# Two gate projections of each merge tile as seven block products, in three of four chunks of a gated mixer layer on one core

## The chip, the cores and the metric

The kernel runs on one core of a Trainium2 chip. Its time is the device time of one execution in microseconds. Three runs of the kernel before gave 2286.47, 2287.43 and 2288.08 us, median 2287.43 us. The engines are named as in the profile: PE is TensorE (PEld its weight loads), DVE is VectorE, ACT is ScalarE, POOL is GpSimd, SP is SyncE, which issues nearly all DMAs here.

## What is computed

One layer over x of 2048 tokens by 1024 channels, all in float32. A norm of the rows, one wide projection, three token mixers (a 31-tap convolution, differential attention with 4 heads, a 3-tap gated convolution), and then the merge, which is the part of this case:

```python
h = rmsnorm(x, norm_g[l])
proj = h @ w_in[l]
(a_val, a_gate, a_z, q, k, v, b_z, c_b, c_c, c_x, c_z, gates) = jnp.split(proj, SPLIT_IDX, axis=-1)
...                       # y_a, y_b, y_c: outputs of the mixers, each (tokens, 1024)
g = jax.nn.sigmoid(gates + gate_b[l]).reshape(b, s, N_BRANCH, D_MODEL)
merged = g[:, :, 0] * y_a + g[:, :, 1] * y_b + g[:, :, 2] * y_c
x = x + merged @ w_o[l]
...
return rmsnorm(x, final_g)
```

The gates are three times 1024 columns of the wide projection, with 1024 channels to sum over.

## The kernel before

Everything is held turned: channels on the 128 partitions, tokens along the row. The 2048 tokens are done in four chunks of 512 (chunk 0 to 3). A product in float32 is made of three products of a faster format: each operand is split into a high part (a rounded copy, by ACT) and a low part (the rest, by DVE or POOL), and high*high, high*low and low*high are summed in one PSUM bank. One weight tile (1024 channels to 128 outputs) is thus 8 blocks of channels by 3 products, 24 matmuls with 512 columns each, in one bank of PSUM.

**Steps.** Each engine runs a program written out by hand over the same clock of steps: 88 weight tiles in a chunk, 6 steps to a tile, 528 steps in a chunk, 4 matmuls of 512 columns to a step (`PARTS`, `SPAN`, L52 to L62). Whatever is to be done at step p stands in each engine's program at step p, and semaphores hold the engines together. The tiles of a chunk are: 44 of the heads (steps 0 to 263, with the attention put in between), 8 of gate a (264 to 311), 8 merge tiles of three weight tiles each (312 to 455, `MID_AT`, 18 steps to each), 4 of y_a (456 to 479, `YA_AT`), 8 of the output projection (480 to 527, `FIN_AT`).

**A merge tile** m makes 128 channels of gate b (24 matmuls), 128 of gate c (24), and then y_b and y_c (12 each, 512 channels to sum over). `row_part` (L790) does the gates into the two banks `PJ`; ACT reads each bank with a tanh into `TG` (`gate`, L1125), and DVE multiplies with the y products and sums into `merged` (`product`, L1615).

**Weights.** In chunk 0 each tile comes raw into `Wraw`, is split by ACT (`split_hi`) and by POOL or DVE (`split_lo`) into one of three slots of `Wp`, and is stored split to DRAM (`store_split`, 1 MB). In the other chunks `load_split` (L616) brings it back, one load of 1 MB for each tile, issued when the tile three before is used up.

**Other work that matters here.** The 124 taps of the long convolution run on DVE, `HEAD_TAPS` (L362) of them spread over steps 40 to 264 and the rest before the layer norm at `LN_AT` (L223). POOL does small powers and a few splits. At `XN_AT` (L236, step 444) the rows of the next chunk are squared by ACT, at `XS_AT` (460) PE spreads their scales, from `XT_AT` (461) on DVE and ACT make the normed and split input `hT`. The rows come in with `load_x` at XN_AT - 8 and XN_AT - 4, into the rooms of `UC` and `SZA`, which the branch of y_a must have left (`za_lo`). Keys and values (`KM`, `VM`) are used by the attention until about step 300 and by the output projection from step 456; the score banks `SC` are free between them.

Of the kernel before, what the change touches and what calls it, by code (L numbers as in the profile page):

```python
# [49 lines left out]
W_SLOTS = 3  # L50
# [17 lines left out]
BANK_CHUNK = G_CHUNK // 2  # L68
# [7 lines left out]
def bank_use(c, r):  # L76

    return BANK_CHUNK * c + r // 2
# [14 lines left out]
def weight_slot(c, i):  # L93
    return (W_CHUNK * c + i) % W_SLOTS


def last_group(i):

    if i < W_MID:
        return i  # L100
    if i < W_YA:
        m, k = divmod(i - W_MID, 3)
        return G_MID + 4 * m + (k if k < 2 else 3)
    return G_YA + 2 * (i - W_YA) + 1

# [94 lines left out]
OSUM_LAG = (10, 10, 10, 9)  # L200
# [9 lines left out]
DIRECT_SPREAD = (19, 15, 15, 15)  # L210
# [12 lines left out]
LN_AT = (408, 408, 408, 414)  # L223
# [6 lines left out]
LN_SPREAD_AT = 13  # L230
# [5 lines left out]
XN_AT = 444  # L236
XS_AT = 460

XT_LOADS = 4
XT_LOAD_AT = 451  # L240
XT_LOAD_STEP = 6
XRES_STEP = 4
XT_AT = 461
# [6 lines left out]
YA_AT = PARTS * W_YA  # L250
FIN_AT = PARTS * W_FIN
# [58 lines left out]
SPARE = 14  # L310
# [27 lines left out]
def room_table(c):  # L338


    free = [(r, None) for r in range(SPARE if c == 0 else 4 * KB)]
# [17 lines left out]
    return room, [(r, done) for p, done, r in gates]  # L359


HEAD_TAPS = (58, 46, 24, 0)  # L362
HEADS_FROM = 40
HEADS_TO = 264
AFTER_FROM = 268
# [54 lines left out]
def build(nc, x, x_t, w_stream, cols, final_g, lam_v, out, kd, vd, ws, rs):  # L420
    with ExitStack() as ctx:
# [17 lines left out]
        xres = PX[:, 1, :, :, :].rearrange("p t m n -> p t (m n)")  # L439
        ZA = sb("ZA", [P, 2, KB, CHUNK], F32R)  # L440
# [6 lines left out]
        Wraw = sb("Wraw", [P, 2, D])  # L447
        Wp = sb("Wp", [P, W_SLOTS, 2, D], F32R)
# [16 lines left out]
        LT = [SZB[:, :], Y[:, :], ACC2, VT]  # L465
        identf = sb("identf", [P, P])
# [33 lines left out]
        w_loaded = [sem(f"w_loaded{k}") for k in range(2)]  # L500
        w_stored = [sem(f"w_stored{k}") for k in range(W_SLOTS)]
        w_back = [sem(f"w_back{k}") for k in range(W_SLOTS)]
# [11 lines left out]
        tanh_done = sem("tanh_done")  # L514

# [42 lines left out]
        def pair_rooms(c):  # L558


            if c > 0:
                return [Wraw[:, 0, k * 2 * P:(k + 1) * 2 * P] for k in range(4)]
            return [room(SPARE + k // 2)[:, k % 2 * 2 * P:(k % 2 + 1) * 2 * P] for k in range(4)]


        OV = Wraw[:, 1, 0:2 * P]
# [18 lines left out]

        def pj(c, r):
            return FIRST_BANKS[r] if c == 0 and r < 2 else PJ[bank(r)]
# [6 lines left out]
        def weight_used(eng, c, i):  # L594

            if i < W_FIN:
                eng.wait_ge(group_done, G_CHUNK * c + last_group(i) + 1)
            elif i < W_CHUNK - 1:
                eng.wait_ge(fin_done, FIN_SIGNALS * c + i - W_FIN + 1)
            else:  # L600
                eng.wait_ge(fin_done, FIN_SIGNALS * (c + 1))
# [4 lines left out]
        def _(sp):  # L606
            def load_raw(w):
                wait(sp, w_lo, w - 1)
                sp.dma_start(Wraw[:, w % 2, :], w_stream[w, :, :]).then_inc(w_loaded[w % 2], 16)

            def store_split(w):
                k = w % W_SLOTS
                sp.wait_ge(w_lo, w + 1)
                sp.dma_start(ws[w, :, :, :], Wp[:, k, :, :].bitcast(F32)).then_inc(w_stored[k], 16)

            def load_split(c, i):  # L616
                k, before = weight_slot(c, i), W_CHUNK * c + i - W_SLOTS
                weight_used(sp, before // W_CHUNK, before % W_CHUNK)
                if before < W_CHUNK:
                    sp.wait_ge(w_stored[k], 16 * (before // W_SLOTS + 1))  # L620
                if c == 1:
                    sp.wait_ge(w_stored[i % W_SLOTS], 16 * (i // W_SLOTS + 1))
                sp.dma_start(Wp[:, k, :, :].bitcast(F32), ws[i, :, :, :]).then_inc(w_back[k], 16)
# [68 lines left out]
            for w in range(W_SLOTS):  # L692
# [1157 lines left out]
```

## Time and profile before

| | |
|---|---|
| median of three runs | 2287.43 us |
| the profiled execution | 2287.08 us, span of its trace 2285.3 us, granted clock 0.999 |
| PE matmul busy | 2258.3 us, 10822 matmuls |
| DVE, ACT, POOL busy | 1425.9, 756.3, 232.9 us |
| DMA | 493.53 MB, mean 216 GB/s |
| chunk 0, 1, 2, 3 begin at about | 14, 540, 1085, 1664 us; the last matmul ends at 2276 |

The page gives busy shares of each engine, the chain of work that ended last, and groups of instructions. Matmuls are pipelined, and so the duration of one (about 390 ns at 512 columns) is longer than the distance from one start to the next; prices of PE are taken from distances.

### The profile page before, as it was taken

The numbers are of one execution on the slowest core, as the hardware profiler recorded it, in microseconds if no ns is written. First come the engines' busy times: TensorE is split into PE (matmuls) and PEld (weight loads), VectorE is DVE, ScalarE is ACT, GpSimd is POOL, SyncE is SP. The second block draws the span as 40 slices with busy tenths as digits, with TensorE's granted clock in tenths as the row PEclk, the third lists the DMA queues.
The fourth block names the chain that finished last, engine by engine and source line by source line (L and its number), as shares of the span: only waits on it lengthen the run. The fifth ranks groups of instructions, "written<-read, shape, count | busy, mean of one in ns | idle before, by whom it ended". The sixth has DMA issues, their size and how long they took to land.

```text
span 2285.3 us, 29046 instructions
## 1 busy us (share of the span) xinstructions
PE 2258.3 (99%) x10822; PEld 1833.4 (80%) x10822; DVE 1425.9 (62%) x2706; ACT 756.3 (33%) x1610; POOL 232.9 (10%) x186
## 2 busy tenths in 40 slices
PE   7999999999999999999999999999999999999998
PEld 6888888878888888888788788888877787788886
DVE  4767667774666675554566667665546656677752
ACT  4334332342333331021344344102135445441121
POOL 3544400100000000010000000001000000000010
PEclk9999999999999999999999999999999999999999
DMA  8877788788566665566655565556775555545555
GB/s 312 287 267 265 269 289 290 273 326 325 163 202 196 180 153 193 200 241 249 258 182 173 171 195 159 169 187 239 262 260 143 174 163 168 158 135 184 187 192 201
DMA packets 99339, 493.53 MB, mean 216 GB/s; under 512 B 15360, under 2 KB 18304, under 8 KB 54144
## 3 DMA queue, kind: packets, MB, share of 16 engines
q1 hardware_dynamic: 90464, 488.90, 63.9%
q10 hardware_dynamic: 8736, 2.78, 0.6%
q8 instruction: 87, 1.43, 0.3%
q14 instruction: 52, 0.43, 0.1%
HBM read 378.37 MB, written 113.27 MB: 215 GB/s over the span
## 4 chain that ended last, share of the span: by engine, by line
PE 95%; DVE 2%; DMA 1%; issue 1%; ACT 1%; SPq 0%; DVEq 0%; ACTq 0%
PE PJ L768 74%; PE SC L827 6%; PE SC L859 5%; PE TB L868 3%; PE OB L892 1%; PE OB L893 1%; PE OB L827 1%; PE PJ L827 1%; PE OB L895 1%; PE OB L894 1%; PE TB L903 0%; DMA PX<-x_t 0%; DMA UC<-x 0%; PE TB L919 0%; DVE Wp L1341 0%
## 5 line engine op out<-in xcount | busy, mean ns | idle before, releaser
L768 PE MATMUL PJ<-hT,Wp 128*128 128x512 f32 x6480 | 1571.6, 394 | 0.5 <-DVE PX L1631 0.5
L768 PEld LDWEIGHTS PJ<-hT,Wp 128*128 128x128 f32 x6480 | 1189.5, 188 | 254.2 <-issue 17.7
L1551 DVE SCALAR_TENSOR_TENSOR ACCS<-UA,col,ACCS 128x512 f32<-128x512 f32 x464 | 350.7, 798 | 0.4
L1065 ACT ACTIVATE PX<-SC,negm 128x512 f32<-128x512 f32 (+3 forms) x320 | 196.2, 623 | 145.7 <-DVE negm L1380 143.8
L1425 DVE TENSOR_TENSOR ZA<-TB,ZA 128x512 fp32r<-128x512 f32 (+1 forms) x144 | 95.1, 661 | 176.9 <-ACT ZA L1085 176.0
L1380 DVE TENSOR_REDUCE negm<-SC 128x2 f32<-128x1024 f32 (+3 forms) x160 | 169.0, 1062 | 40.2 <-PE SC L859 37.6
L1085 ACT ACTIVATE ZA<-TB 128x512 fp32r<-128x512 f32 (+1 forms) x144 | 82.7, 574 | 322.1 <-PE TB L868 322.1
L1136 ACT ACTIVATE TG<-PJ,col 128x512 f32<-128x512 f32 x64 | 44.1, 689 | 348.1 <-PE PJ L768 348.0
L1418 DVE SCALAR_TENSOR_TENSOR PX<-PX,sc 128x512 f32<-128x512 f32 (+3 forms) x160 | 108.1, 696 | 51.0 <-ACT PX L1076 50.8
L827 PE MATMUL SC<-Wp,KM 128*128 128x512 f32 x384 | 121.4, 389 | 0.0
L1076 ACT ACTIVATE PX<-PX,sc 128x512 f32<-128x512 f32 (+3 forms) x160 | 98.9, 655 | 64.9 <-DVE sc L1407 44.6
L1245 POOL TENSOR_TENSOR Wp<-Wraw,Wp 128x1024 fp32r<-128x1024 f32 x42 | 106.2, 2529 | 126.6 <-ACT Wp L990 126.6
L859 PE MATMUL SC<-KM,ZA 64*128 64x512 f32 (+3 forms) x960 | 118.5, 379 | 0.0
L990 ACT ACTIVATE Wp<-Wraw 128x1024 fp32r<-128x1024 f32 x88 | 92.8, 1055 | 59.8 <-DMA Wraw<-w_stream 34.6
L859 PEld LDWEIGHTS SC<-KM,ZA 64*128 64x128 f32 x960 | 80.3, 184 | 39.2 <-issue 28.7
L768 PE MATMUL PJ<-ZC,Wp 128*128 128x512 f32 x384 | 93.2, 390 | 2.5 <-ACT TG L1136 2.5
L768 PE MATMUL PJ<-ZB,Wp 128*128 128x512 f32 x384 | 92.7, 390 | 0.0
L768 PE MATMUL PJ<-ZA,Wp 128*128 128x512 f32 x384 | 89.1, 391 | 1.7 <-DVE CT L1631 0.9
L768 PEld LDWEIGHTS PJ<-ZC,Wp 128*128 128x128 f32 x384 | 71.8, 188 | 17.7 <-issue 2.9
L768 PEld LDWEIGHTS PJ<-ZA,Wp 128*128 128x128 f32 x384 | 71.6, 188 | 17.5 <-DVE Wp L1341 2.0
L768 PEld LDWEIGHTS PJ<-ZB,Wp 128*128 128x128 f32 x384 | 72.1, 188 | 15.4 <-issue 0.5
L827 PEld LDWEIGHTS SC<-Wp,KM 128*128 128x128 f32 x384 | 72.1, 188 | 14.9
(192 smaller groups left out, 2038.5 us busy)
## 6 DMA issues: line engine op xcount, KB each, us to landing
Wp<-split_weights SPq DMA_DIRECT2D x264, 1024.0 KB, 4.8
split_weights<-Wp SPq DMA_DIRECT2D x88, 1024.0 KB, 4.9
Wraw<-w_stream SPq DMA_DIRECT2D x88, 512.0 KB, 5.9
KM<-keys SPq DMA_DIRECT2D x24, 512.0 KB, 5.9
VM<-values SPq DMA_DIRECT2D x24, 512.0 KB, 6.4
PX<-x SPq DMA_DIRECT2D x16, 512.0 KB, 7.8
out<-PX SPq DMA_DIRECT2D x16, 512.0 KB, 10.6
keys<-KM SPq DMA_DIRECT2D x12, 512.0 KB, 9.6
```

Of the source, the lines that this page charges most:

```text
L768: mm = pe.matmul(pj(c, r)[:, :], wt, rhs[:, 1 if q == 1 else 0, k, :], start=(n == 0), stop=(n == 3 * ktiles - 1))
L827: mm = pe.matmul(FIN_BANKS[half][t], (mTl if q == 1 else mTh)[:, k, t * P:(t + 1) * P], Wp[:, weight_slot(c, w), 1 if q == 2 else 0, kk * ...
L859: mm = pe.matmul(SC[k][:, m, 0:w], QM[rows, ql, t * P:(t + 1) * P], KM[rows, kl, j * CHUNK:j * CHUNK + w], start=(n == 0), stop=(n == 2))
L990: act.activation(Wp[:, k, 0, :], Wraw[:, w % 2, :], ACT.Copy).then_inc(w_hi, 1)
L1065: a = act.activation(probs(c, h, t, j, m)[:, 0:w], SC[k][:, m, 0:w], ACT.Exp, bias=negm[:, t % 2, j, m:m + 1], accum_out=lsum[:, t % 2, j, ...
L1076: act.activation(probs(c, h, t, j, 0)[:, 0:w], probs(c, h, t, j, 0)[:, 0:w], ACT.Copy, scale=sc[:, t % 2, j, 0:1]).then_inc(half_done, 1)
L1085: act.activation(AT[:, u % 2, 0, 0:w], TB[:, 0:w], ACT.Copy).then_inc(at_hi, 1)
L1245: pool.tensor_tensor(Wp[:, k, 1, :], Wraw[:, w % 2, :], Wp[:, k, 0, :].bitcast(F32), ALU.subtract).then_inc(w_lo, 1)
L1380: dve.tensor_reduce(negm[:, t % 2, j, :], SC[k][:, :, 0:w], AX.X, ALU.max, negate=True).then_inc(negm_ready, 1)
L1418: dve.scalar_tensor_tensor(out=probs(c, h, t, j, 0)[:, 0:w], in0=probs(c, h, t, j, 1)[:, 0:w], scalar=sc[:, t % 2, j, 1:2], in1=probs(c, h ...
L1425: dve.tensor_tensor(AT[:, u % 2, 1, 0:w], TB[:, 0:w], AT[:, u % 2, 0, 0:w].bitcast(F32), ALU.subtract).then_inc(tb_free, 1)
L1551: a = dve.scalar_tensor_tensor(out=acc, in0=src, scalar=col[:, n:n + 1], in1=acc, op0=ALU.mult, op1=ALU.add)
```

## The change

For chunks 1 to 3 the two gates of a merge tile are one product of a 2 by 2 block matrix of weights (two gates by two halves of the 1024 channels) with a 2 by 2 block matrix of the input (two halves of the channels by two halves of the 512 tokens). It is now made of seven block products in place of eight (Winograd's form): each product is 4 blocks of channels by 3 splits, 12 matmuls of 256 columns. Four of the seven need sums of weight blocks (S1 to S4), four need sums of blocks of the input. Chunk 0 keeps the plain products.

- PE: `gates_part`, 7 matmuls of 256 columns to a step in place of 4 of 512; the products lie in the score banks. y_b and y_c are as before.
- DVE: `add_quarter`, seven adds of 128x256 for each merge tile, with one operand in PSUM, into `TG`; ACT copies the first product to SBUF (`copy_first`), and the tanh reads `TG`.
- Weight sums: in chunk 1, steps 24 to 272, 32 sums: DVE adds 128x512, ACT and POOL split, SP stores 512 KB each to `wsum`; raw weights are loaded for it (256 KB halves).
- Weight blocks: slots are halves now (six of 512 KB); S1 to S4 and y come back as 512 KB loads, the three plain blocks of each merge tile come raw (256 KB) and are split by ACT and POOL. Chunk 0 no longer stores the 16 gate tiles.
- Sums of the input: steps 508 to 519 of chunks 0 to 2: DVE four adds and four splits of 1024 elements to a partition, ACT four copies; stored (2 x 2 MB) at steps 20 and 40 of the next chunk, loaded back into the rooms of keys and values after the attention (at 272 and about 305), in pieces of 256 elements.
- Places: layer norm of chunk 0 at 400, of chunk 3 at 408 (before 408 and 414); norm of the next input at 452 in chunk 0 and 448 in the next two (before 444), its spread at 468 in chunk 0; more taps among the heads in chunks 1 to 3.

```diff
-LN_AT = (408, 408, 408, 414)
+LN_AT = (400, 408, 408, 408)
-LN_SPREAD_AT = 13
+LN_SPREAD_AT = 15
-XN_AT = 444
-XS_AT = 460
+XN_AT = (452, 448, 448, 0)
+XS_AT = (468, 460, 460, 0)
-XT_LOAD_AT = 451
+XT_LOAD_AT = (459, 451, 451, 0)
-XT_AT = 461
+XT_AT = (469, 461, 461, 0)
+RAW_AT = ((0, 0, -14), (0, 1, -13), (1, 1, -9))
+SPLIT_AT = ((A11, -6), (A12, -5), (A22, 0))
+QUARTER_AT = (6, 7, 7, 10, 10, 12, 12)
+BLOCK_AT = ((S1, -9), (S2, -7), (S3, -3), (S4, 0), (YB, 4), (YC, 6))
+SUM_AT = 24
+SUM_STEP = 8
+SUMS_AT = 508
+SUMS_STORE_AT = (20, 40)
+X_LOAD_AT = (442, 444)
+SUMS_BACK_AT = 272
-HEAD_TAPS = (58, 46, 24, 0)
+HEAD_TAPS = (58, 72, 78, 50)
...
+            def store_sum(m, k):
+                sp.wait_ge(sum_lo, 4 * m + k + 1)
+                sp.dma_start(wsum[m, SUM_ORDER[k], :, :, :], SS[:, :, :].bitcast(F32)).then_inc(sum_stored, 16)
...
+            def load_block(c, m, k):
+                q, i = mid_block(m, k), W_MID + 3 * m + 2
+                s = block_slot(c, q)
+                slot_free(sp, c, q)
...
+                sp.dma_start(Wp[:, s, :, :].bitcast(F32), src).then_inc(w_back[s], 16)
...
+            def load_sums(c, k):
+                if k == 0:
+                    sp.wait_ge(qk_done, units_before(c + 1))
+                else:
+                    sp.wait_ge(pv_done, turns_before(c + 1))
...
+                for half in range(2):
+                    a = slice(HALF * half, HALF * (half + 1))
+                    for l in range(2):
+                        sp.dma_start((TS, TU)[k][:, l, :, a].bitcast(F32), tz[k if half == 0 else 1 - k, :, l, :, a]
+                                     ).then_inc(t_back[k], 16)
...
+            def gates_part(c, m, part):
+                n0 = merge_at(c, m)
+                for n in range(PRODUCTS * part, PRODUCTS * (part + 1)):
+                    b, i = divmod(n, 3 * KB)
+                    k, q = divmod(i, 3)
+                    if i == 0:
+                        weight_ready(c, mid_block(m, b))
...
+                        elif b == S3:
+                            pe.wait_ge(p1_copied, n0 + 1)
+                            if m == 0:
+                                pe.wait_ge(t_back[1], 64 * c)
+                        elif b == S4:
+                            pe.wait_ge(quarter_done, PRODUCTS * n0 + 1)
+                        elif b == A22:
+                            pe.wait_ge(quarter_done, PRODUCTS * n0 + 3)
...
+                    mm = pe.matmul(P_BANKS[b], Wp[:, block_slot(c, mid_block(m, b)), 1 if q == 2 else 0, k * P:(k + 1) * P], rows,
+                                   start=(i == 0), stop=(i == 3 * KB - 1))
...
+            def block_hi(c, m, b):
+                q, half = mid_block(m, b), raw_of(m, b)
+                slot_free(act, c, q)
+                raw_loaded(act, c, *half)
+                act.activation(Wp[:, block_slot(c, q), 0, :], raw_home(c, *half), ACT.Copy).then_inc(w_hi, 1)
+            def sum_high(m, k):
+                act.wait_ge(sum_ready, 4 * m + k + 1)
+                wait(act, sum_stored, 16 * (4 * m + k))
...
+                act.activation(SS[:, 0, :], sum_home(m, SUM_ORDER[k]), ACT.Copy).then_inc(sum_hi, 1)
+            def copy_first(c, m):
...
+                act.activation(P1[:, :], P_BANKS[A11], ACT.Copy).then_inc(p1_copied, 1)
...
+            def add_quarter(c, m, k):
+                n = merge_at(c, m)
+                b, src, dst, after = ((S2, P1[:, :], C22, 0), (S1, C22, C12, 1), (A12, P1[:, :], C11, 0), (S3, C22, C21, 1),
+                                      (S1, C21, C22, 4), (S4, C12, C12, 2), (A22, C21, C21, 4))[k]
+                dve.wait_ge(prod_done, PRODUCTS * n + b + 1)
...
+                dve.tensor_tensor(dst, P_BANKS[b], src, ALU.add).then_inc(quarter_done, 1)
...
-                        if p == MID_AT + MID_STEPS * m + PARTS:
+                        if p == MID_AT + MID_STEPS * m + (PARTS if c == 0 else 2 * PARTS - 1):
                             gate(c, m, 1)
...
+                        for k in range(4):
+                            if c == 1 and p == SUM_AT + SUM_STEP * (4 * m + k):
+                                weight_sum(m, k)
+                    for n in range(4):
+                        if c + 1 < NCHUNK and p == SUMS_AT + 2 * n:
+                            turned_sums(c + 1, n)
+                        if c + 1 < NCHUNK and p == SUMS_AT + 5 + 2 * n:
+                            sums_lo(c + 1, n // 2, n % 2)
```

The store of a weight sum stands in SP's program five steps after DVE's sum, ACT's copy and POOL's rest one step after it, the next sum eight steps after it.

## Rows read from the trace of the kernel before

**Rows 1.** The page, parts 1 and 2: busy time, and TensorE's clock in 40 slices.

```profile
PE 2258.3 (99%) x10822; PEld 1833.4 (80%) x10822; DVE 1425.9 (62%) x2706; ACT 756.3 (33%) x1610; POOL 232.9 (10%) x186
...
PEclk9999999999999999999999999999999999999999
```

**Rows 2.** The page, part 4: the chain that ended last, by engine.

```profile
PE 95%; DVE 2%; DMA 1%; issue 1%; ACT 1%; SPq 0%; DVEq 0%; ACTq 0%
```

**Rows 3.** Waits of PE, whole span: us in total, times, longest us.

```profile
PE TB L839 <- DVE SZB L1353: 8.8, 3, 7.8
PE OB L768 <- DVE hT L1369: 3.3, 2, 2.6
PE PJ L768 <- ACT TG L1136: 2.5, 1, 2.5
...
PE PJ L768 <- DVE Wp L1341: 0.8, 1, 0.8
```

**Rows 4.** The chain in order of time: a piece of chunk 1's merge stage.

```profile
887.59 85.24 PE PJ L768 x376
```

**Rows 5.** Timeline of PE: 256-column matmuls of the attention and what follows (start, us).

```profile
595.63 0.28 PE L894 MATMUL OB<-ZA,VM 128*128 128x256 f32 x1
...
595.86 2.01 PE L768 MATMUL PJ<-hT,Wp 128*128 128x512 f32 x8
...
2065.87 0.28 PE L894 MATMUL OB<-ZA,VM 128*128 128x256 f32 x1
...
2066.11 2.91 PE L768 MATMUL PJ<-hT,Wp 128*128 128x512 f32 x12
```

**Rows 6.** Timeline of PE's weight loads around such a pair.

```profile
1726.58 0.19 PEld L895 LDWEIGHTS OB<-ZA,VM 128*128 128x128 f32 x1
1726.69 1.69 PEld L768 LDWEIGHTS PJ<-hT,Wp 128*128 128x128 f32 x8
```

**Rows 7.** Timeline: end of chunk 0, load of rows, the two engines behind it.

```profile
458.01 2.31 SPq L630 DMA_DIRECT2D UC<-x  x2
...
466.45 1.06 ACT L995 ACTIVATE ACCS<-UC 128x1024 f32<-128x1024 f32 x1 [4.59 <-DMA UC<-x]
...
467.50 0.67 ACT L1136 ACTIVATE TG<-PJ,col 128x512 f32<-128x512 f32 x1
```

**Rows 8.** Groups by form, whole span: busy us, mean ns of one.

```profile
L1551 DVE SCALAR_TENSOR_TENSOR ACCS<-UA,col,ACCS 128x512 f32<-128x512 f32 x464 | 350.7, 798 | 0.4
...
L1431 DVE TENSOR_TENSOR Wraw<-Wraw,OB 128x256 f32<-128x256 f32 x24 | 10.1, 420 | 27.3 <-ACT Wraw L1094 27.1
...
L1276 POOL TENSOR_TENSOR ZA<-UC,ZA 128x512 fp32r<-128x512 f32 x16 | 23.8, 1501 | 58.4 <-ACT ZA L1152 58.4
```

**Rows 9.** Windows: PE, PEld, DVE, ACT, POOL busy (instructions), clock, DMA share, GB/s.

```profile
540.00:842.00 302.00, 302.00 (x1499) 244.77 (x1499) 189.69 (x432) 102.62 (x261) 16.88 (x20) 1.00 0.63 195
...
1664.00:2040.00 376.00, 375.64 (x1970) 298.12 (x1969) 238.10 (x501) 181.40 (x454) 19.76 (x21) 1.00 0.56 173
889.00:1020.00 131.00, 131.00 (x579) 107.64 (x578) 73.72 (x131) 22.16 (x37) 9.53 (x10) 1.00 0.58 211
...
1020.00:1042.00 22.00, 22.00 (x103) 18.36 (x102) 18.58 (x29) 6.33 (x10) 0.00 (x0) 1.00 0.74 264
```

**Rows 10.** Timeline, chunk 0: a POOL split and a tiny DVE operation beside it.

```profile
105.38 2.49 POOL L1245 TENSOR_TENSOR Wp<-Wraw,Wp 128x1024 fp32r<-128x1024 f32 x1 [4.73 <-ACT Wp L990]
...
105.72 2.16 DVE L1410 TENSOR_TENSOR sc<-Lr,lamv 128x2 f32<-128x2 f32 x1
```

**Rows 11.** The line of the 512 KB stores values<-VM, whole span.

```profile
DMA to landing us min/median/max: 3.4/4.5/8.5
```

**Rows 12.** DMA issues in 1004 to 1022 us: us to landing.

```profile
UC<-x SPq DMA_DIRECT2D x2, 512.0 KB, 7.4
```

**Rows 13.** Timeline, heads of chunk 1: turned weights ready on DVE, and PE's use.

```profile
628.35 0.69 DVE L1425 TENSOR_TENSOR ZA<-TB,ZA 128x512 fp32r<-128x512 f32 x1 [2.94 <-ACT ZA L1085]
...
631.17 0.39 PE L892 MATMUL OB<-ZA,VM 128*128 128x512 f32 x1
```

## What the change will do to the time: the prediction

> **What bounds the kernel now.** I read the page first. TensorE is busy for 99% of the span at the full clock (2.4 GHz) in every slice, DVE for 62% [rows 1], and 95% of the chain that ended last is TensorE [rows 2]. A chain of one engine has two ways to get shorter: fewer starts, or fewer waits. So the next view is the list of TensorE's waits: 8.8 us of DVE's first scales, nearly all of it at the start of the program, 3.3 us for the first rows, and then, in over 2250 us, only some 5 us, most of it one wait of 2.5 us and one of 0.8 us at the end of chunk 0 [rows 3]. The time is therefore the sum of TensorE's start distances, and a saved matmul is saved time unless a new wait takes its place. All sums below are made against the profiled execution, 2287.08 us (its span is 2285.3); the median of the three runs is 2287.43, 0.35 us above it, so that no correction is made.
>
> **Price of a matmul.** At 512 columns, from the chain in the merge stage of chunk 1: 85.24 us / 376 = 0.2267 us from start to start [rows 4]. At 256 columns the trace has pairs in the attention (lines 894 and 895), followed at once by a projection. From the start of line 894 to that of the projection, two starts on, are 0.23 us at the first of them and 0.24 at the last; of 108 such pairs 64 show 0.24 and 44 show 0.23, a mean of 0.2359, so 0.1180 us for one [rows 5]. That is more than half of 0.2267 (0.1134). Each needs its own weight load, and the loads of such a pair begin 0.11 us apart though each is shown with 0.19 [rows 6]: loads overlap each other, and 0.118 can be held in a long row of them, for which the trace has no example beyond a pair.
>
> **Term 1, the products.** Removed in each merge tile: 48 matmuls of 512 columns, 48 x 0.2267 = 10.88 us. Added: 84 of 256, 84 x 0.1180 = 9.91 us. Gain 0.97 us, in 8 tiles of 3 chunks: 24 x 0.97 = 23.3 us, all of it on the path. One eighth of the arithmetic is gone (24 x 1.36 = 32.6 us at half price), but nearly a third of that goes back for the narrower form. Bounds: 0.1134 us (half of the wide one) gives 32.6 us; 0.1226 us, as far above the mean as the half lies below it, gives 24 x (10.88 - 10.30) = 13.9 us.
> The Trainium skill (TensorE: Matmul & The Clock Gate, section Back-to-back issue gap) puts the distance at columns / 2.4 GHz plus 2.5 ns, so 109 ns and 216 ns. By it the term would be 24 x (48 x 0.2158 - 84 x 0.1092) = 28.5 us; the rows show 10 ns more at either width, and the sum above doesn't use the rule.
>
> **Term 2, the end of chunk 0.** The load of the last two row tiles was issued at 458.01, ScalarE waited for it until 466.45, and the tanh of a gate queued behind it began at 467.50 [rows 7]; this is TensorE's wait of 2.5 us, and 0.8 us follow on a late weight split [rows 3]. With the squares eight steps later (7 us) and the layer norm eight earlier, the load has 12 steps (11 us) from issue to use in place of 8, against 8.4 us seen. Gain 3.3 us (0 to 4.2, the last with the two waits of 0.5 us on products in the same place).
>
> **Term 3, what is added, and its cover.**
> DVE's adds. Seven of 128x256 with one operand in PSUM, 0.42 us each (line 1431 has this form) [rows 8], 2.9 us in a merge tile. Per chunk 56 x 0.42 = 23.5 us; out of the stage go 26, 54 or 50 taps of 0.80 us (21, 43, 40 us), so its sum on DVE grows by 3 us in chunk 1 (to some 76 of 124 us) and falls in the others [rows 8, 9]. TensorE waits for the adds only at the sixth product (first add, at step 6, used at 8.6) and the seventh (third add, step 7, used at 10.3), about 2 us of room. That suffices outside the layer norm. At steps 423 to 435 DVE has in addition four applies (1.2 us each) and four products (1.4 to 1.5 us each), with the adds of tile 6 some 14 us of work in 10 us: it falls behind by about 4 us, and the third add of tile 6 comes perhaps 0.5 us late. 3 x 0.5 = 1.5 us (0 to 6).
> POOL's splits. Three of 128x512 in each merge tile, 1.5 us each [rows 8], and 32 in the heads of chunk 1. Beside a POOL operation a DVE operation on two numbers took 2.16 us, until POOL was done [rows 10]. If half of a split's length falls on DVE, that is 24 x 0.75 = 18 us in a merge stage, in all 94 of 124 us in chunk 1, 76%. The stage of y_a ran at 18.58 of 22 us, 84%, with no wait of TensorE in chunk 1 [rows 9]. So no more than the 1.5 us above.
> The Trainium skill (GPSIMD Engine Reference, section Specifications) says that POOL shares its SBUF interfaces with VectorE and contends with DVE instructions that have two SBUF inputs. The row agrees, and the rule speaks against this change, which moves some 150 us of splits to POOL; the adds themselves have one input in PSUM and would by it be delayed only behind others.
> Start of the merge stage. The third and fourth sum blocks of the input come in 2 MB of 1 KB pieces, issued at about step 305 once the attention is done, and wanted at 319, 12 us later. A pair of 512 KB loads took 8.4 us in the dense place [rows 7], four of them between 8 and 17 us: a wait of 0 to 5 us in each chunk, of which I take 0.5, since the DMA share at that point is far below the dense place. 3 x 0.5 = 1.5 us (0 to 12). SP's queue behind it (weight blocks S2, S3) has about 8 to 10 steps of room.
> End of the merge stage in chunks 1 and 2. SP reaches step 444 with the load of the first y_a tile, whose slots come free only with the fifth product of tile 7 (step 446.6). Behind it in SP's queue stand the block of y_c (wanted at step 453) and two row tiles (squared from 452, spread fixed at 460, where before there were eight steps of room more). A row tile took 7.4 us to land [rows 12], 9 steps: 446.6 + 9 = 456, and square, power and diagonal take 3 us more. So TensorE waits 0 to 3 us, I take 1: 2 x 1 = 2 us (0 to 6).
> Heads of chunk 1. DVE gets 32 sums and 26 taps, 58 x 0.80 = 46 us on 189.7: 236 of 302 us, 78%, with half of POOL's 32 splits 86% [rows 9]. ScalarE gets 32 copies and a wait for the store of the sum before (the slower rival). I take 1.5 us (0 to 10). Chunks 2 and 3 get 54 and 50 taps more there; 238 + 40 = 278 of 376 us is 74%, I take nothing (0 to 3).
> Sums of the input at steps 508 to 519: 10 us of DVE work in some 20 us of steps that were a third busy, and no user in TensorE before the merge stage; their stores have 8 us of cover. Nothing.
> Sum of term 3: 1.5 + 1.5 + 2 + 1.5 = 6.5 us.
>
> **Forecast.** 2287.08 - 23.3 - 3.3 + 6.5 = 2267.0 us.
>
> **Rivals.**
> A, the clean one: a long row of narrow matmuls runs at half the wide distance, and all new waits are hidden. 2287.08 - 32.6 - 3.3 = 2251.2 us. For it: the engine moves half the columns. Against: 108 pairs at 0.118 [rows 5].
> B, waits take the place: the adds or the weight blocks come late in every merge tile, not in one. At 0.7 us in each tile 24 x 0.7 = 16.8 us in place of the 1.5 at the layer norm: 2267.0 + 15.3 = 2282.3 us. For it: chains of two engines in 2 us of room, DMA traffic of the stage up from 3 to 3.75 MB a tile. Against: shares of 76% and less.
> C, slower, by one mechanism: in the heads of chunk 1 ScalarE's copy of a weight sum waits until the store of the one before has landed. It has 4 steps of 302 / 264 = 1.14 us, 4.6 us. ScalarE's queue holds behind it the copies of turned weights, whose DVE half is done at 629.04 and used at 631.17, 2.1 us of room [rows 13]. A store that lands after more than 6.7 us thus costs TensorE the rest, 32 times. Like stores took 3.4 to 8.5 us, median 4.5 [rows 11], at a DMA share of 0.63, which the sums raise to about 0.63 x (195 + 79) / 195 = 0.89 (24 MB in 302 us) [rows 9]. At 8.5 us for all: 32 x 1.8 = 58 us, 2267.0 - 1.5 + 58 = 2323 us. It decides against the change from a mean landing of 6.7 + 21.6 / 32 = 7.4 us on.
> D, the moved norm only shifts the stall: chunk 0 keeps its 3.3 us and the spread at 460 waits 3 us in chunks 1 and 2: 2267.0 + 3.3 + 4 = 2274.3 us.
>
> **How the numbers follow.** Forecast 0.55, A 0.12, B 0.13, C 0.08, D 0.12. Leaving out most of C and the outer half of A, the range is 2255 to 2281 us; it takes in D and most of B, and the bounds 13.9 and 32.6 us of term 1 alone give 2258 to 2276. About 0.2% (4.6 us) is what a measurement of this kernel can tell from no change. Faster by more: forecast, A, D and most of B, 0.87. Within: the rest of B and a mild C, 0.06. Slower by more: C, 0.07.
>
> **What would show it.** Distances in the merge stage: 0.118 from start to start over a whole product, stages of chunks 1 to 3 about 8 us shorter. TensorE's waits: the 2.5 us for ScalarE gone; small ones on DVE's adds in tile 6 of a chunk, on the load of the sums at step 319, on the scales at step 460. In the heads of chunk 1 ScalarE idle before the copies of sums with the store as releaser, short. The forecast is wrong if the narrow distance is above 0.1226, or if chunk 1's heads are longer by more than 5 us.

## The result and the profile after

| | kernel before | changed kernel |
|---|---|---|
| median of 5 | 2287.51 us (2286.47 to 2288.24) | 2300.40 us (2297.05 to 2306.08) |
| ratio, 95% interval | | 1.0062 [1.0051, 1.0072] |
| profiled execution | 2287.08 us, span 2285.3 | 2306.08 us, span 2304.3 |

The change makes the kernel 0.6% slower; the prediction was 2267.0 us, range 2255 to 2281. The profiled execution of the changed kernel is the longest of the five, 5.7 us above their median, so the parts found below add up to some 19 us more than before, not to 13. Two executions of later kernels ran in a slower state (3169.08 us with two rooms, 2768.86 us with the burst spread, granted clock 0.66 and 0.75) and are in no median; the second was the profiled one, so that kernel has no profile to compare.

The page of the changed kernel, to be held against [rows 1, 2]: busy time, the clock in 40 slices, the chain.

```profile
PE 2255.8 (98%) x11686; PEld 1864.3 (81%) x11686; DVE 1572.8 (68%) x2930; ACT 830.9 (36%) x1750; POOL 382.4 (17%) x290
PEclk9999999999999999999999999999999999999999
...
PE 84%; DMA 8%; DVE 5%; issue 1%; ACT 1%; POOL 1%; SPq 0%; ACTq 0%; DVEq 0%; POOLq 0%
```

TensorE held 95% of the chain before; now 84%, and 8% is DMA. The list of TensorE's waits (us in total, times, longest), against [rows 3]:

```profile
PE PJ L1081 <- DMA Wp<-split_weights: 11.0, 8, 3.2
PE TB L1192 <- DVE SZB L1837: 9.5, 3, 7.8
PE OB L1245 <- DVE ZA L1909: 8.9, 5, 2.5
PE OB L1081 <- DVE hT L1853: 3.3, 2, 2.5
PE TB L1256 <- ACT PX L1491: 3.2, 2, 2.0
PE PJ L1081 <- DVE CT L2118: 0.8, 1, 0.8
PE SC L1212 <- DVE KM L1963: 0.7, 1, 0.7
```

Rows two and four are the start of the program, as before. New are 11.0 us for weight blocks, 8.9 us for turned weights (the attention's probabilities, turned for its second product), and 3.2 us for ScalarE. The products themselves behave as forecast in kind. The chain in chunk 1's merge stage (start, us, what), against [rows 4]:

```profile
906.34 8.38 PE SC L1120 x70
914.73 5.47 PE PJ L1081 x24
920.19 10.07 PE SC L1120 x84
930.27 5.47 PE PJ L1081 x24
```

A row of 84 narrow matmuls takes 10.07 us, 0.1199 us each, with no gap; 48 wide ones took 10.88. That is 0.81 us for each tile and 19.4 us for 24 (forecast 0.97 and 23.3), all of it on the path as forecast. But the place after which the piece of 906.34 begins stands at 887.59 in [rows 4]: the merge stage of chunk 1 begins 18.75 us later, although chunk 0 ended 3.4 us earlier (its first product of the output stage is at 492.91 instead of 496.30). So the heads of chunk 1 lost 22.1 us, more than all 24 merge tiles bring.

**Why the heads lose.** The copy of a weight sum on ScalarE (L1359) and the store of the sum before it (L867), each line's own view:

```profile
L1359 ACT ACTIVATE ZA<-Wraw x32: 617/632/648, 561.7 to 862.0; 128x512 fp32r<-128x512 f32 x32
its engine sat idle before it (us, times) until:
  DMA split_sums<-ZA: 73.4, 15
...
L867 SPq DMA_DIRECT2D split_sums<-ZA x32: 319/320/3381, 563.7 to 867.2; - x32
...
DMA to landing us min/median/max: 2.6/5.2/14.1
```

Half of the 31 copies that follow a store wait for it, 4.9 us in the mean. The timeline shows what one such wait does (rows of SP's queue, ScalarE, VectorE and TensorE):

```profile
668.76 0.32 SPq L867 DMA_DIRECT2D split_sums<-ZA  x1
...
676.99 3.90 PE L1081 MATMUL PJ<-hT,Wp 128*128 128x512 f32 x16
680.51 0.63 ACT L1359 ACTIVATE ZA<-Wraw 128x512 fp32r<-128x512 f32 x1 [8.16 <-DMA split_sums<-ZA]
681.04 0.58 ACT L1472 ACTIVATE ZA<-TB 128x512 fp32r<-128x512 f32 x1
...
681.65 0.69 DVE L1909 TENSOR_TENSOR ZA<-TB,ZA 128x512 fp32r<-128x512 f32 x1 [3.94 <-ACT ZA L1472]
...
682.40 0.50 PE L1245 MATMUL OB<-ZA,VM 128*128 128x512 f32 x1 [1.51 <-DVE ZA L1909]
...
682.74 0.39 PE L1246 MATMUL OB<-ZA,VM 128*128 128x512 f32 x1
```

The store issued at 668.76 lands 11.7 us later. The copy waits 8.16 us for it, behind it in ScalarE's queue stands the copy of turned weights (L1472), its other half on VectorE (L1909) follows, and TensorE waits 1.51 us. This is rival C of the prediction, row for row. It costs a little more than the list says. After 16 starts at a distance of 0.2267 us the product of L1245 would have begun at 676.99 + 3.63 = 680.62; it began at 682.40, 1.78 us late, and the one behind it 0.34 us later, not 0.23. So each wait costs some 0.4 us beyond its listed length here (an estimate from this row; the waits at 640.94 and 764.85 give the same).

**Why the merge stage ends late.** SP's queue and TensorE in tile 7 of chunk 1:

```profile
1019.72 0.90 SPq L918 DMA_DIRECT2D SZA<-x  x2
1023.70 0.33 SPq L877 DMA_DIRECT2D Wp<-split_weights  x1
1024.12 1.29 SPq L892 DMA_DIRECT2D Wp<-split_weights  x1
...
1026.35 2.91 PE L1081 MATMUL PJ<-ZB,Wp 128*128 128x512 f32 x12
1032.14 4.61 PE L1081 MATMUL PJ<-ZC,Wp 128*128 128x512 f32 x12 [2.88 <-DMA Wp<-split_weights]
```

SP stands at the y_a tile's load (L877) until a product has freed its slots, at 1023.70, and issues the y_c block (L892) only behind it. The block was wanted at 1029.1 (12 starts after 1026.35) and landed about 8 us after its issue. The row also shows a second cost: the same 12 matmuls that took 2.91 us in the row above take 4.61 us after the wait. The windows of 20 us (PE, PEld, DVE, ACT, POOL busy; then clock, DMA share, GB/s) name the reason:

```profile
580.00:600.00 20.00, 17.70 (x81) 13.85 (x80) 13.90 (x29) 6.40 (x16) 2.56 (x2) 0.91 0.93 345
720.00:740.00 20.00, 17.89 (x84) 14.57 (x85) 16.41 (x32) 8.32 (x21) 5.01 (x4) 0.91 0.75 281
...
1600.00:1620.00 20.00, 16.83 (x83) 14.14 (x82) 7.66 (x31) 5.82 (x10) 5.54 (x7) 0.83 0.84 317
```

The granted clock is 0.91 in five windows behind waits of 2 to 3 us (also 860, 1020 and 2100 us) and 0.83 in one: part of the time at 1.2 GHz instead of 2.4. 9% of 20 us are 1.8 us. So this wait of 2.9 us costs 2.9 + 1.7 = 4.6 us.

### The profile page after: what moved, and what is told of

It is laid out like the page before. It is cut to its first block, busy times and chain, and to the rows that moved or that the text cites. A ratio compares the mean times of both kernels' runs of the same rounds, so it can differ in the third digit from the quotient of the medians.

```text
span 2304.3 us, 32147 instructions
## 1 busy us (share of the span) xinstructions
PE 2255.8 (98%) x11686; PEld 1864.3 (81%) x11686; DVE 1572.8 (68%) x2930; ACT 830.9 (36%) x1750; POOL 382.4 (17%) x290
## 4 chain that ended last, share of the span: by engine, by line
PE 84%; DMA 8%; DVE 5%; issue 1%; ACT 1%; POOL 1%; SPq 0%; ACTq 0%; DVEq 0%; POOLq 0%
PE PJ L1081 55%; PE SC L1120 10%; PE SC L1180 6%; DMA split_sums<-ZA 4%; PE SC L1212 4%; DMA Wp<-split_weights 2%; PE TB L1221 2%; PE OB L1245 1%; PE OB L1246 1%; PE PJ L1180 1%; PE OB L1180 1%; PE OB L1248 1%; PE OB L1247 1%; DVE PX L1902 1%; PE TB L1256 0%
## 5 line engine op out<-in xcount | busy, mean ns | idle before, releaser
L1081 PE MATMUL PJ<-hT,Wp 128*128 128x512 f32 x5328 | 1307.5, 396 | 1.9 <-DMA Wp<-split_weights 1.9
L1081 PEld LDWEIGHTS PJ<-hT,Wp 128*128 128x128 f32 x5328 | 975.9, 189 | 210.5 <-issue 15.4
L2035 DVE SCALAR_TENSOR_TENSOR ACCS<-UA,col,ACCS 128x512 f32<-128x512 f32 x464 | 381.0, 837 | 0.8
L1909 DVE TENSOR_TENSOR ZA<-TB,ZA 128x512 fp32r<-128x512 f32 (+1 forms) x144 | 94.9, 659 | 161.0 <-ACT ZA L1472 160.5
L1472 ACT ACTIVATE ZA<-TB 128x512 fp32r<-128x512 f32 (+1 forms) x144 | 82.4, 573 | 281.1 <-PE TB L1221 281.1
L1667 POOL TENSOR_TENSOR Wp<-Wraw,Wp 128x512 fp32r<-128x512 f32 x66 | 99.1, 1501 | 245.7 <-ACT Wp L1352 243.2
L1902 DVE SCALAR_TENSOR_TENSOR PX<-PX,sc 128x512 f32<-128x512 f32 (+3 forms) x160 | 113.4, 725 | 34.0 <-ACT PX L1463 33.7
L1120 PE MATMUL SC<-hT,Wp 128*128 128x256 f32 x864 | 117.3, 284 | 0.0
L1120 PEld LDWEIGHTS SC<-hT,Wp 128*128 128x128 f32 x864 | 110.4, 191 | 4.0 <-issue 1.6
L1081 PE MATMUL PJ<-ZC,Wp 128*128 128x512 f32 x384 | 99.9, 410 | 9.8 <-DMA Wp<-split_weights 9.1
```

The source lines that it names most:

```text
L1081: mm = pe.matmul(pj(c, r)[:, :], Wp[:, block_slot(c, q0 + k // KB), 1 if q == 2 else 0, k % KB * P:(k % KB + 1) * P], rhs[:, 1 if q == 1 e ...
L1120: mm = pe.matmul(P_BANKS[b], Wp[:, block_slot(c, mid_block(m, b)), 1 if q == 2 else 0, k * P:(k + 1) * P], rows, start=(i == 0), stop=(i = ...
L1667: pool.tensor_tensor(Wp[:, s, 1, :], raw_home(c, *raw_of(m, b)), Wp[:, s, 0, :].bitcast(F32), ALU.subtract).then_inc(w_lo, 1)
L1902: dve.scalar_tensor_tensor(out=probs(c, h, t, j, 0)[:, 0:w], in0=probs(c, h, t, j, 1)[:, 0:w], scalar=sc[:, t % 2, j, 1:2], in1=probs(c, h ...
L1909: dve.tensor_tensor(AT[:, u % 2, 1, 0:w], TB[:, 0:w], AT[:, u % 2, 0, 0:w].bitcast(F32), ALU.subtract).then_inc(tb_free, 1)
L2035: a = dve.scalar_tensor_tensor(out=acc, in0=src, scalar=col[:, n:n + 1], in1=acc, op0=ALU.mult, op1=ALU.add)
```

## The experiments

Each is timed in 5 to 11 executions, against the kernel before on the same chip (2286.7 to 2287.0 us each time). The theory: the heads of chunk 1 lose their time through ScalarE's wait for the store of a sum (rival C), the rest is lost where SP's queue holds a weight block back, and the low clock makes each wait dearer. The rivals: the work of the sums itself (32 adds on VectorE, 32 copies, 32 splits on GpSimd) is what the heads can't hold; or narrow products are worth less than the chain shows.

**Two rooms for the stores.** The sums are split into two places in turn, each with its own semaphore, so that a copy waits for the store before the last.

```diff
-        SS = ZA[:, 0, 2:4, :]
+        SUM_ROOMS = [ZA[:, 0, 2:4, :], UC[:, 2:4, :].bitcast(F32R)]
...
-                wait(act, sum_stored, 16 * (4 * m + k))
+                wait(act, sum_stored[k % 2], 16 * (2 * m + k // 2))
```

> The weight sums of chunk 1 are split into two rooms in turn (the second is UC's last two heads, unused at that time), so that ScalarE's copy of a sum waits for the store of the sum before the last, 12 steps after its issue in place of 4. All the work stays. Theory (ScalarE waits for the store of a sum, and with it the turned weights of the attention): ScalarE's 73 us of waits for these stores fall below 5 us, TensorE's waits for the DVE half of the turned weights (8.9 us) and for the squares (3.2 us) go, with the spells of low clock behind them; chunk 1's heads get shorter by 15 to 22 us, 2278 to 2285 us in all against 2300. Rival (DVE's 58 added operations make the turned weights late): ScalarE's waits go, TensorE's stay, 2297 us or more. Rival (the DMA queues are full, share 0.87): the wait moves to the weight tiles, 2292 us or more.

Measured: 2285.62 us, ratio 0.9996 [0.9987, 1.0005], 14.8 us under the changed kernel; the theory's range ended at 2285. ScalarE waits for no store any more, and yet the stores land later than in the changed kernel, 8.3 us in the median instead of 5.2. The line of the store in this kernel:

```profile
L868 SPq DMA_DIRECT2D split_sums<-ZA x16: 319/326/3301, 564.0 to 838.9; - x16
L868 SPq DMA_DIRECT2D split_sums<-UC x16: 319/327/633, 573.2 to 848.8; - x16
...
DMA to landing us min/median/max: 2.6/8.3/15.9
```

With no engine waiting for them, the transfers follow each other faster: the DMA share in the heads is 0.90 (537 to 887 us), against 0.87 (537 to 904 us). TensorE's list has 0.4 us left on the turned weights, and the weight blocks as they were:

```profile
PE PJ L1084 <- DMA Wp<-split_weights: 11.7, 6, 3.2
...
PE OB L1248 <- DVE ZA L1915: 0.4, 1, 0.4
```

The traffic and all the work of the sums are the same: what cost time was the wait for the store, not the load nor the work.

**No sums.** The weight sums are left out: no adds, copies, splits and stores of sums in chunk 1, and the blocks S1 to S4 are read from the y weights instead.

```diff
-                    src = wsum[m, k, :, :, :]
+                    src = ws[i, :, k % 2, :, :]
```

> Leaves out the weight sums of chunk 1 altogether (32 sums on DVE, their copies on ScalarE, rests on POOL, loads of raw weights and stores of 512 KB); the four sum blocks of each merge tile are loaded from another weight tile of the same size, so that the matmuls and all loads of the merge stages stay. It bounds what the sums cost by any way. Theory: chunk 1's heads lose all of the 22 us by which they are longer than the even gain, 2278 us, and e1 comes within 5 us of it. Rival (the taps moved among the heads and the stores of the turned sums make chunk 1 longer): 2290 us or more.

Measured: 2284.55 us, ratio 0.9992 [0.9983, 1.0001]. The theory's 2278 was missed by 6.5 us. TensorE still waits 13.4 us for weight blocks, 5.1 us of it once, at 861.7 us, with a window of 0.91 behind it; that long wait makes the comparison of whole times (1.1 us less than with the sums and two rooms) a weak one. The stage itself can be compared. The table has the heads of chunk 1, from their first product to the first of the merge stage, in the profiled executions (in the kernel before the end is 8 starts before 887.21), the waits of TensorE listed in them, and what the clock took:

| kernel | heads, us | waits | clock | rest |
|---|---|---|---|---|
| before | 345.6 | 0 | 0 | 345.6 |
| changed | 367.6 | 13.4 | 5.4 | 348.8 |
| two rooms | 350.5 | 3.3 | 0 | 347.2 |
| two rooms, SP's order mended (below) | 353.5 | 4.9 | 1.8 | 346.8 |
| the fastest version (below) | 348.0 | 1.6 | 0 | 346.4 |
| no sums | 352.5 | 5.1 | 1.8 | 345.6 |
| no sums, SP's order mended (below) | 349.3 | 3.3 | 0 | 346.0 |

With the waits and the clock taken off, the stage is less than 2 us longer with the sums than without them, and the 0.4 us that each wait costs besides makes most of that (three or four waits in the versions with sums and two rooms, one in those without). So the work of the sums costs next to nothing, and the rival falls.

**One step less between sums.** The changed kernel with one number changed.

```diff
-SUM_STEP = 8
+SUM_STEP = 7
```

> The changed kernel with one number changed: a weight sum every 7 steps instead of every 8, so that the copy of the next sum stands 3 steps behind the store of the one before, not 4. Theory (the copy on ScalarE waits for that store, and TensorE pays what goes beyond the room): each of the 15 or so late stores costs up to one step of 1.14 us more: 2309 us (2303 to 2316), ScalarE's wait for the stores above 85 us. Rival: what costs time in the heads of chunk 1 is the work of the sums on VectorE, ScalarE and GpSimd itself; with 31 steps less over which it is spread the sum of that work is the same: within 2 us of the changed kernel, 2298 to 2302.

Measured: 2324.79 us, ratio 1.0158 [1.0142, 1.0175], 24.4 us over the changed kernel. The sign and ScalarE's wait (86.9 us in 18 waits, from 73.4 in 15) are as expected, the size is nearly three times what was. TensorE's waits grew by some 14 us, as much as ScalarE's:

```profile
PE OB L1245 <- DVE ZA L1909: 17.8, 7, 5.3
PE PJ L1081 <- DMA Wp<-split_weights: 13.1, 5, 3.5
...
PE PJ L1081 <- DVE SZB L1984: 4.1, 1, 4.1
```

TensorE's wait of 4.1 us for VectorE's SZB is new, and it begins at the same copy:

```profile
590.54 0.63 ACT L1359 ACTIVATE ZA<-Wraw 128x512 fp32r<-128x512 f32 x1 [7.79 <-DMA split_sums<-ZA]
...
594.67 1.75 PE L1081 MATMUL PJ<-hT,Wp 128*128 128x512 f32 x4 [4.14 <-DVE SZB L1984]
```

ScalarE's work for VectorE stands behind the copy, VectorE sits idle for 7.69 us until 591.60, and its product SZB, which frees TensorE's bank, starts at 593.85. And over 537 to 904 us the granted clock was 0.96, about 14 us, where the changed kernel has three windows of 0.91 in its heads, 5.4 us. The expectation had counted neither what stands behind the copy at each place nor the clock.

**SP's order at the end of the merge stage.** The y_a tile's load moves from step 444 to 447, behind the y_c block, and in chunks 2 and 3 the two raw halves of tile 1 that stood before the y_c block of tile 0 move behind it.

```diff
-                        elif i < W_CHUNK and c > 0 and not merge_tile(i):
+                        elif i < W_CHUNK and c > 0 and not merge_tile(i) and i != W_YA:
                             load_split(c, i)
+                    if c > 0 and p == PARTS * (W_YA - 2) + 3:
+                        load_split(c, W_YA)
...
-                                if s == at:
+                                if s == (at if c == 1 or m != 1 or i > 0 else -11):
```

> SyncE's order alone: the load of the first y_a tile is issued at step 447 in place of 444 and so stands behind the block of y_c of the last merge tile and the rows of the next chunk; in chunks 2 and 3 the two raw halves of merge tile 1, which wait for the last split of the attention's output, stand behind the block of y_c of merge tile 0. Nothing is added or left out. Theory (SyncE is blocked by a wait and the y_c block behind it is issued late): TensorE's waits for weight blocks before y_c of 2.9, 3.2, 2.1 and 0.9 us go, with the low clock behind them of about 1.8 us each, 10 to 16 us in all: 2285 to 2290 us. Rival (the blocks are late because the DMA engines are full at the end of the merge stage): the waits stay or move to the y_a tile, 2297 us or more.

Measured: 2290.83 us, ratio 1.0017 [1.0009, 1.0026], 9.6 us under the changed kernel and 0.8 over the theory's range. The waits for weight blocks fell from 11.0 us in 8 to this, and those for the turned weights stayed:

```profile
PE OB L1247 <- DVE ZA L1911: 8.6, 5, 2.8
PE PJ L1083 <- DMA Wp<-split_weights: 4.5, 3, 2.4
```

The y_c block is no longer late. Two of the three waits left (2.4 us at 1031.63 and 1.4 at 1606.89) are for the y_a tile, so the rival came in part.

**Both together.**

> e1 and e4 together. Theory: the two costs are independent, 2300 - 18 - 13 = 2269 us, faster than the kernel before by 0.8%; what is left is 24 merge tiles shorter by 0.8 us each and the 3.4 us of chunk 0. Rival (one of the costs hides the other, since waits taken away in one place come back at the next): above 2280 us.

Measured: 2279.57 us, ratio 0.9967 [0.9954, 0.9979]: faster than the kernel before, but 10 us over the expectation. What is left can be read off. The output stage of chunk 0 begins at 493.75 instead of 496.30, so 2287.08 - 19.4 - 2.6 = 2265.1 us; the waits from there on (7.2 us for weight blocks, 1.1 for turned weights, 1.1 in three others) and the clock in four windows (0.91, 0.91, 0.95, 0.97 of 20 us, 5.2 us) make 2279.7. The profiled execution took 2282.79; the 3.1 us between are close to what seven waits cost besides, at 0.4 us each. The three long waits have two causes. At 864.50 us:

```profile
843.37 2.49 SPq L912 DMA_DIRECT2D KM<-turned_sums  x4
...
864.50 4.34 PE L1086 MATMUL PJ<-hT,Wp 128*128 128x512 f32 x12 [3.13 <-DMA Wp<-split_weights]
```

Four loads of 512 KB were issued within 2.5 us, 21 us before; the weight tile issued behind them at 848.89 landed after 15.6 us. The kernel without sums has this wait too. At 1020.77 and 1597.25 us the y_a tile is late, because its load now stands behind row tiles 2 and 3, which wait 4 us on SP for their room.

**The burst spread.**

```diff
-                    if c > 0 and p == SUMS_BACK_AT:
-                        load_sums(c, 0)
+                    for n in range(4):
+                        if c > 0 and p == SUMS_BACK_AT + 4 * n:
+                            load_sums(c, 0, n)
```

> The kernel with two rooms and the mended order, with the four 512 KB loads of the turned sums at steps 272, 276, 280 and 284 instead of all at step 272. Theory: the burst of 2 MB in 2.5 us is what let a weight tile land late at 864.5 us (wait 3.13 us, then matmuls at the lower clock in that window): both go, in each later chunk nothing changes; 2274.7 us (2273 to 2277), no window under 1.00 between 840 and 900 us. Rival: the share of the DMA engines there is full anyway and the wait stays, at another tile: 2279.6 us.

Measured: 2277.25 us, ratio 0.9956 [0.9943, 0.9969]. That is 2.3 us under the version before it, of 4.9 expected, and with the two intervals overlapping the time alone doesn't show it. The next version is the same program up to this place, and there the wait of 3.13 us is one of 1.07 at 860.05 us, with no window under 1.00. That speaks for the burst and doesn't prove it: with the burst in place the same wait took 1.41 us in the kernel with two rooms, 3.13 here, 3.35 and 5.10 in the two without sums, one trace of each, and the spread gave a single one.

**Rows of the next input later in chunks 1 and 2 as well.**

```diff
-XN_AT = (452, 448, 448, 0)
-XS_AT = (468, 460, 460, 0)
+XN_AT = (452, 452, 452, 0)
+XS_AT = (468, 468, 468, 0)
...
-X_LOAD_AT = (442, 444)
+X_LOAD_AT = (442, 448)
```

(and the transposed loads and sums 8 steps later too)

> The one before, and in chunks 1 and 2 the places of chunk 0 for the next input: loads of rows 2 and 3 at step 448 behind the y_a tile's load (it stood behind their wait of 4 us on SyncE), norms at 452, squares at 468, transposed loads from 459. Theory: the y_a tile lands before its first matmul in merge tile 7, so the waits of 1.96 and 2.11 us near 1020 and 1597 us go, with the lower clock in three windows behind them (about 1.8 us each): 2267.5 us (2265 to 2271). Rival: the later transposed loads are paid at the head of the next chunk, as rival D has it: within 2 us of the run before it.

Measured: 2271.69 us, ratio 0.9935 [0.9924, 0.9947], 0.65% faster than the kernel before and 0.7 us over the theory's range. TensorE's waits, apart from the start of the program and three of 0.2 us:

```profile
PE PJ L1091 <- DVE CT L2133: 1.7, 2, 0.9
PE PJ L1091 <- DMA Wp<-split_weights: 1.1, 1, 1.1
PE SC L1130 <- DMA Wp<-split_sums: 0.8, 1, 0.8
PE PJ L1091 <- ACT TG L1545: 0.7, 1, 0.7
PE OB L1255 <- DVE ZA L1922: 0.3, 1, 0.3
```

No window between the start and 2260 us is under 1.00. The first and the fourth of these rows lie in chunk 0, whose output stage begins at 494.04, 2.3 us earlier than before. So 2287.08 - 19.4 - 2.3 = 2265.4 us, and 2.8 us of waits after it make 2268.2, against the profiled execution's 2270.20: within 2 us nothing else is left. The forecast of 2267.0 is nearly met here, but partly by offsetting errors: the products bring 3.9 us less than it took, and the waits are fewer than its 6.5 us.

**The same with one room.** The step back that tells whether the second room is needed once all else is spread.

> The fastest version so far (2271.69 us) with one room for the stores of weight sums again. Theory: the second room is worth by itself what it brought on the changed kernel, 14.8 us: 2286.5 us (2282 to 2292), with ScalarE waiting 60 us or more for the stores. Rival: with the other loads spread the stores land sooner and the room matters little: 2272 to 2276 us.

Measured: 2288.09 us, ratio 1.0005 [0.9996, 1.0014]: 16.4 us for the one room, as the theory had it. The heads of chunk 1 take 365.5 us, with 15.0 us of TensorE's waits in them and no window under 1.00, so the one room costs this much even when the clock doesn't fall. The spread loads didn't make the stores land sooner (median 6.0 us, longest 15.6), and ScalarE waits as before:

```profile
  DMA split_sums<-ZA: 82.7, 17
...
PE OB L1252 <- DVE ZA L1916: 8.8, 10, 1.8
```

**No sums, with SP's order mended.**

> Weight sums of chunk 1 left out (blocks S1 to S4 are read from the y weights, so the output isn't the reference's), and SyncE's order at the end of the merge stage mended: the y_a tile's load at step 447, raw halves of tile 1 in chunks 2 and 3 behind the y_c block. Theory: what is left of the change is the seven products, the turned rows and chunk 0; of the 13.4 us of weight-block waits seen without sums some 6 go, with 3 us of low clock behind them: 2275 us (2270 to 2279). Rival: the products themselves give less than the 19.5 us read from the pitch, and the waits only move: 2282 to 2285 us, with the sum of TensorE's waits below 8 us.

Measured: 2279.01 us, ratio 0.9968 [0.9957, 0.9979], from 2274.77 to 2286.45, a wide spread for this kernel. The median is at the upper end of the theory's range, 7.0 us of waits for weight blocks are left. The kernel with the sums, two rooms and the same order took 2279.57 us: here too leaving out the sums brings nothing that can be told apart. Of the products it says no more than that they bring at least this.

**Chunk 0's places alone,** on the kernel before.

```diff
-LN_AT = (408, 408, 408, 414)
+LN_AT = (400, 408, 408, 414)
...
-XN_AT = 444
-XS_AT = 460
+XN_AT = (452, 444, 444, 0)
+XS_AT = (468, 460, 460, 0)
```

> The kernel before with the last part of the change alone: in chunk 0 the layer norm of the gates 8 steps earlier and the norm, squares and transposed loads of the next chunk's input 8 steps later, and nothing else. Theory (term 2 of the prediction; the changed kernel's final stage of chunk 0 began 3.4 us earlier than before's): 2283.5 us, 3.3 us under the kernel before, and TensorE's wait of 2.5 us on the tanh near 468 us gone. Rival: the load only lands as late for another reason, or the later norm is paid at the head of chunk 1 (v of its first head later): within 1 us of the kernel before.

Measured: 2285.68 us, ratio 0.9994 [0.9985, 1.0003], 1.2 us less. The wait of 2.5 us on the tanh is gone, and another has come:

```profile
476.15 7.36 PE L768 MATMUL PJ<-ZA,Wp 128*128 128x512 f32 x24 [2.64 <-DVE CT L1631]
```

VectorE stood 3.10 us at a weight split whose copy by ScalarE was late, and a merge behind it; the granted clock is 0.92 in the window behind. The copy had itself waited 3.67 us for its raw weights, issued at 465.97 and landed about 7 us later. In the changed kernel the same load lands about 4.6 us after its issue at 466.51, the split waits 1.02 us (at 472.18) and TensorE not at all at this place. There chunk 0 no longer stores its 16 gate tiles, and the DMA share from 300 to 460 us is 0.52, here 0.82; that this is why the load lands sooner is likely and wasn't tried.

## Why the prediction was wrong, by its steps

From 2267.0 to the profiled 2306.08 us are 39.1 us:

- **Price of a narrow matmul (term 1): right in kind, the gain sized too large.** 0.1199 us in a long row, not the 0.1180 of a pair: 19.4 us instead of 23.3, 3.9 us of the miss. It lies between the bounds, 13.9 and 32.6. The formula in the Trainium skill (TensorE: Matmul & The Clock Gate, section Back-to-back issue gap), which that section gives for a single matmul on its own and not for a long stream, makes 109 ns, 11 ns under what this trace shows.
- **End of chunk 0 (term 2): 3.4 us in the changed kernel, as said,** but 1.2 us when made alone. The step was that the wait goes and nothing is late next; alone, a weight split was late next. The 3.4 us in the changed kernel thus hang on something the term didn't name, most likely the lighter DMA traffic of its chunk 0, and that they met the forecast is in part luck.
- **Heads of chunk 1 (term 3): the step that failed.** The prediction took 1.5 us for ScalarE's wait for the store and for VectorE's load, with 10 as its bound; 22.1 us were lost, 20.6 us of the miss. The mechanism stood on record as rival C, with a chance of 0.08 and a point of decision, a mean landing of 7.4 us. What was held against it was a wrong reading: "Like stores took 3.4 to 8.5 us, median 4.5 [rows 11], at a DMA share of 0.63". These 12 stores lie in three chunks, and the view of [rows 11] by chunk has them apart (0 to 540 us, then 540 to 1085 us):

```profile
DMA to landing us min/median/max: 6.7/7.1/8.5
...
DMA to landing us min/median/max: 3.4/4.5/4.6
...
20.00:264.00 244.00, 244.00 (x1160) 199.64 (x1160) 154.39 (x264) 94.51 (x176) 116.51 (x54) 1.00 0.81 278
```

The four of chunk 0 ran at a DMA share of about 0.81 (the last row, 20 to 264 us) and took 7.4, 6.7, 6.8 and 8.5 us, 7.35 in the mean; only the eight later ones belong to a share near 0.63. The prediction worked out 0.89 for the changed kernel, and 0.87 to 0.90 came. So the trace of before already had landings at the point of decision, at a lower share than the one to come. With nothing waiting the stores then took 8.5 us in the mean (two rooms, median 8.3; 8.9 and 9.4 in the two faster versions).

Rival C wasn't right in its size either. Its price of 58 us was for 8.5 us on all 32. In the changed kernel the waits thin out the traffic, the median is 5.2 us and the mean 6.6, below the 7.4 us, and 22 us were lost all the same: the landings scatter from 2.6 to 14.1 us, and 14 of the 32 take more than 6.7, which a mean doesn't show. Nor does each of these cost what goes beyond 6.7 us; the one shown above landed after 11.7 us and gave a wait of 1.51. Of the 22.1 us the waits listed in the heads make 13.4 and the clock 5.4; the 3.3 left are about what ten waits cost besides their listed length, at the 0.4 us estimated above.

- **End of the merge stage (term 3): right place, wrong waiter and size.** The prediction saw SP stand at the y_a tile and listed the y_c block and the row tiles behind it, then priced only the row tiles: "0 to 3, I take 1". The y_c block, wanted 3 steps earlier, was the late one: 2.88 us in chunk 1 and 3.2 in chunk 2, and with the clock behind them 4.6 and 6.6 (one window at 0.83, 3.4 us), together 9.2 us over the 2 taken. Chunk 3 had 0.9 us of the same and 2.14 us with a clock window in its first tile, whose y_c block SP issued at 2104.43, behind raw loads: 4.9 us that no step had.
- **The clock: left out altogether.** The prediction sums waits as if each cost its own length. Behind each of its six waits of about 2 us or more the changed kernel lost another 1.7 us or, once, 3.4, some 12 us in all (contained in the items above). This was the profiled execution, the longest of five; how much of it another one loses isn't shown.
- **DVE's adds in tile 6, and the start of the merge stage: not seen.** No wait on either in the list; 3.0 us were taken for them.
- The items add to 3.9 - 0.1 + 20.6 + 9.2 + 4.9 - 3.0 = 35.5 us of the 39.1; 3.6 us stay open. Four short waits that no item holds (at 1139.71, 1701.20, 1964.62 and 2183.39) make 1.8 of them. Rival B (adds late in each tile) and rival D (spread at 460 late) didn't come.

Of the signs named for a wrong forecast the second, "chunk 1's heads longer by more than 5 us", was the one that came.

## What to carry to other kernels

When a step is made to wait for a transfer, take the landing times at the DMA share that the changed kernel will have; here the median was 4.5 us near 0.63, 7.1 at 0.81 and, with nothing waiting for the stores, 8.3 at 0.90. A view over the whole span mixes such stages, so ask for it stage by stage, and look at the spread beside the median. Here a second room for the store (512 KB of space that was free in that stage) was worth 15 to 16 us. Read the queue that issues the loads entry by entry past the one that blocks, and price the first that is wanted. On a kernel that TensorE fills, a wait of about 2 us or more can cost nearly twice its length by the lower clock behind it, though it doesn't each time.

## What was not expected of the hardware

A store of 512 KB landed after 2.6 to 15.9 us within one stage. When the engines no longer waited for the stores, these took longer: the median rose from 5.2 to 8.3 us with the second room. And the granted clock fell after a single wait in a full kernel: after 2.88 us of waiting 12 matmuls of 512 columns took 4.61 us instead of 2.91. It is not the same each time. The eleven traces that can be compared have 34 waits of TensorE of 1.95 us or more after the start of the program, and the granted clock fell behind 22 of them. Length alone doesn't decide it: a wait of 1.96 us before 860.75 had a window of 0.91 behind it, one of 3.35 us before 860.92 in the kernel without sums and with the mended order had none. What does decide wasn't tried.
